# Last two down projections by column halves, the last but one scattered and fetched back in halves

## The chip, the cores and the metric

The kernel runs on one core of a Trainium2 chip, as one program. The metric is device time in microseconds (us), the median over several executions; lower is better. Work is spread over TensorE (PE), VectorE (DVE), ScalarE (ACT) and GpSimd (POOL). SyncE (SP) and POOL issue most of the DMA transfers between DRAM and on-chip memory.

## The reference, cut to what matters

One layer of a hybrid backbone over 128 context and 512 latent tokens of width 1024, all float32. Only its last part, a hierarchical mixture of experts and the final norm, is touched:

```python
# x: (640, 1024) after the mixer; h2 = rmsnorm(x) * (1 + scale2) + shift2
# w_dense (640, 16): top-1 group of 4 experts, then top-2 experts in the group
a = einsum('nd,edf->nef', h2, w_exp_gate)      # 16 experts, 1024 -> 512
u = einsum('nd,edf->nef', h2, w_exp_up)
act = silu(a) * u * w_dense[..., None]
x = x + gate2 * einsum('nef,efd->nd', act, w_exp_down)   # 512 -> 1024
y = rmsnorm(x, g_final)
```

## The kernel before, in words

**Experts.** The 16 experts are visited in the order `expert_at(p)`, p = 0 to 15. Each takes up to 128 tokens (`SLOTS`), gathered by POOL from DRAM (`h2scr`) with an indirect DMA (`gather`). float32 products are made of three products of split numbers (`three`): each weight chunk of 128x2048 is split into a high part by ScalarE (`expert_hi`) and a low part by VectorE (`expert_lo`). An expert has six chunks: four for gate and up (`half`), two for the down projection (`down`), each 1 MB from DRAM. Chunk i can be split once PE has finished chunk i-4. The high copy of p = 15's last chunk (number 95) is the last `expert_hi` of the kernel; the last `expert_lo` follows it on VectorE.

**Down projection.** `down(p)` has FT = 4 blocks of 128 rows. Per chunk (two blocks) it makes 12 products of 128x512: for each block and each of three split products, first the left 512 output columns and then the right 512. So both column halves of the result end together, after the second chunk. `inner_T` of the last expert (a transposition through PE, then `inner_hi` on ScalarE and `inner_lo` on VectorE) is placed between the two chunks of `down(14)`. The result lies in two PSUM banks; ScalarE copies all 128x1024 of it to `yb` (`rows_out`).

**Results.** The result of p = 0 to 14 goes from `yb` to DRAM (`yscr`) by an indirect DMA from POOL (`scatter`). The rows of `yscr` for each token's lower expert are read back as `rowA`, in one transfer of 2.5 MB that POOL issues at p = 13 (line 690). The rows of the upper expert are read back as `rowB` by SP in five transfers of 512 KB (line 549), once the scatter of p = 14 has landed. The result of p = 15 is not needed from DRAM: PE multiplies it with a selection matrix `oh_T` (`last_rows`) and adds `rowB` by an identity product (`second_rows`), tile by tile, t = 0 to 4.

**Tail.** Each engine works through its own queue in the order in which the code writes it, and stops at a wait. ScalarE scales `rowA` by a token weight (`scale_rows`, line 1092). VectorE multiplies it by `gate2` (`base`, line 2011) and adds it to `xr` (`base_add`, line 2016): ten instructions over five tiles, which follow `inner_lo(15)`. Then `combine(t)` (lines 2022, 2025) adds what PE made, ScalarE makes the norm's factor and `finish(t)` (line 2031) applies it; SP writes the tile out.

**ScalarE's order near the end**: `expert_hi(92)`, `(93)`, `tanh_gate(15)`, `inner_hi(14)`, `expert_hi(94)`, `expert_hi(95)`, two copies into `oh_T` (lines 1125, 1126), `inner_hi(15)`, then a wait for the token weights and for `rowA` (`d_ga`), `scale_rows` of t = 0 and 1, `rows_out(14)`, `scale_rows` of t = 2 to 4, `rows_out(15)`.

Of the kernel before, what the change touches and what calls it, by code (L numbers as in the profile page):

```python
# [14 lines left out]
I32 = mybir.dt.int32  # L15
# [5 lines left out]
P = 128  # L21
# [187 lines left out]
def layer_kernel(nc, x_d, small_d, wst_d, wg_d, wpool_d, st_d, rcnt_d,  # L209
                 wexp_d, xt_d, gf_d, bv_d, y_d, so_d, mo_d):  # L210
    ctx = ExitStack()
    with ctx:
# [166 lines left out]
        thr = at("thr", 206, [P, 8])  # L379
        slot_rows = at("slot_rows", 206.0625, [P, 2, NE], I32)  # L380
# [18 lines left out]
        def f32(t):  # L399
# [37 lines left out]
        e_hi, e_lo, e_mm, e_th, e_act, e_part, e_aTp, e_aTh, e_aTl, e_xT, e_xgh, e_xgl, e_y = (  # L437
            sem(n) for n in ("e_hi", "e_lo", "e_mm", "e_th", "e_act", "e_part", "e_aTp", "e_aTh",
# [4 lines left out]
        g_sent, f_ps, s_lt = sem("g_sent"), sem("f_ps"), sem("s_lt")  # L443
        a_steps, v_steps, g_steps = sem("act_steps"), sem("dve_steps"), sem("pool_steps")
# [28 lines left out]
        def _(sp):  # L473
# [47 lines left out]
            with sp.Fori(0, last_round) as r:  # L521
# [40 lines left out]
        def _(gp):  # L562
# [94 lines left out]
            def scatter(r, p):  # L657
                if p:
                    gp.wait_ge(d_sc, r * (16 * NE) + 16 * p)
                    gp.sem_inc(y_sent, 1)  # L660
                if p == NE - 1:
                    for t in range(NT):
                        gp.wait_ge(d_gb[t], (r + 2) * 16)
                gp.wait_ge(e_y, r * NE + p + 2)
                gp.sem_inc(p_go, 1)
                e = expert_at(p)
                gp.indirect_dma_start(yscr, bass.IndirectOffsetOnAxis(
                    ap=slot_rows[:, 1, e:e + 1], axis=0), yb[p % 2][:, :], None).then_inc(d_sc, 16)
                if p == NE - 2:
# [29 lines left out]
        def _(act):  # L699
# [360 lines left out]
            with act.Fori(0, last_round) as r:  # L1060
# [28 lines left out]

                def scale_rows(ts):  # L1090
                    for t in ts:
                        act.activation(rowA[:, t, :], rowA[:, t, :], ACT.Copy,
                                       scale=wab[:, 0, t:t + 1]).then_inc(f_a, 1)

                for t in range(NT):
                    act.wait_ge(d_gb[t], (r + 1) * 16)
# [8 lines left out]
                for p in range(NE):  # L1105
# [8 lines left out]
                    expert_hi(c + 2)  # L1114
                    expert_hi(c + 3)
# [40 lines left out]
        def _(dve):  # L1156
# [682 lines left out]
            with dve.Fori(0, last_round) as r:  # L1839
# [126 lines left out]
                for p in range(NE):  # L1966
# [98 lines left out]
        def _(pe):  # L2065
# [509 lines left out]
            with pe.Fori(0, last_round) as r:  # L2575
# [58 lines left out]
                def down(p, between=None):  # L2634
                    pe.wait_ge(e_aTl, r * NE + p + 1)
                    if p < NE - 1:
                        pe.wait_ge(e_y, r * NE + p + 1)
                    for c in range(2):
# [9 lines left out]
                        if between is not None and c == 0:  # L2648
                            between(p + 1)

                pe.wait_ge(e_y, r * NE + 1)
# [34 lines left out]
                down(NE - 2, inner_T)  # L2686
                down(NE - 1)
# [9 lines left out]
            def second_rows(t):  # L2697
                pe.wait_ge(d_gb[t], rounds * 16 + 16)
# [144 lines left out]
```

## Time and profile before

| | |
|---|---|
| median of 3 runs | 946.25 us (945.71 to 946.47) |
| the profiled execution's own time | 948.32 us |
| its span in the profile | 946.3 us |
| PE busy | 924.8 us, 98% of the span |
| VectorE, ScalarE, GpSimd busy | 746.2, 498.0, 78.8 us |
| granted PE clock, mean | 0.993 of full speed |

The span runs from the first to the last instruction of one profiled execution; the execution's own time is 2.0 us more than it. All times below are us from the span's start.

### The profile page before, as it was taken

How to read it: one execution, taken by the hardware profiler on the slowest of the kernel's cores; microseconds unless marked ns; L12 is line 12 of the kernel's file. 1: busy time of each engine (PE TensorE's matmuls, PEld its weight loads, DVE VectorE, ACT ScalarE, POOL GpSimd, SP SyncE). 2: the span in 40 equal slices, each digit the busy share in tenths (PEclk: the TensorE clock that was granted, in tenths of full speed). 3: DMA queues.
4: the chain of work that ended last, by engine and by line, in shares of the span. 5: the costliest groups of instructions: out<-in, count | busy, mean ns of one | idle time of the engine just before them, and what ended most of it. 6: DMA issues, size and time to landing. Idle time of an engine off the chain costs nothing.

```text
span 946.3 us, 14234 instructions
## 1 busy us (share of the span) xinstructions
PE 924.8 (98%) x5550; PEld 815.4 (86%) x5550; DVE 746.2 (79%) x1038; ACT 498.0 (53%) x660; POOL 78.8 (8%) x91
## 2 busy tenths in 40 slices
PE   7999999999999999999999999989999999999996
PEld 5799999899888999999999998868888888888872
DVE  5798889897494478889464465489999999999998
ACT  5464343343133356576312232257887887887873
POOL 0010110100001010101000000011112111111110
PEclk9999999999999999999999999999999999999998
DMA  9916675574656242434392136179999999999965
GB/s 367 357 60 193 216 231 204 177 266 157 223 198 210 82 127 76 139 124 149 135 358 77 62 125 275 68 257 411 397 422 421 420 407 422 418 410 414 397 265 201
DMA packets 41458, 234.63 MB, mean 248 GB/s; under 512 B 4560, under 2 KB 5008, under 8 KB 20912
## 3 DMA queue, kind: packets, MB, share of 16 engines
q1 hardware_dynamic: 26928, 180.12, 49.5%
q0 software_dynamic: 10720, 44.32, 13.2%
q10 hardware_dynamic: 3744, 9.28, 2.6%
q8 instruction: 44, 0.72, 0.3%
q14 instruction: 22, 0.18, 0.1%
HBM read 208.43 MB, written 25.28 MB: 247 GB/s over the span
## 4 chain that ended last, share of the span: by engine, by line
PE 92%; DVE 4%; DMA 2%; ACT 1%; issue 1%; SPq 0%; DVEq 0%; POOLq 0%; ACTq 0%
PE ps L2067 86%; PE ps L2127 2%; PE ps L2588 1%; DMA raw<-in_wst 1%; PE ps L2630 1%; PE ps L2114 1%; DMA xg<-h2scr,slot_rows 0%; PE ps L2314 0%; PE ps L2425 0%; DVE rowA L2022 0%; DVE xr L2025 0%; DVE xr L2031 0%; PE ps L2502 0%; DVE RP L1359 0%; ACT ghi L774 0%
## 5 line engine op out<-in xcount | busy, mean ns | idle before, releaser
L1848 DVE TENSOR_TENSOR wlo<-raw,whi 128x2048 fp32r<-128x2048 f32 x32 | 72.5, 2289 | 4.2 <-ACT whi L1066 4.0
L1848 DVE TENSOR_TENSOR olo<-raw,ohi 128x2048 fp32r<-128x2048 f32 x32 | 72.4, 2287 | 3.9 <-ACT ohi L1066 3.9
L2067 PE MATMUL ps<-Thi,ghi 128*128 128x320 f32 x224 | 71.1, 317 | 0.0
L1066 ACT ACTIVATE whi<-raw 128x2048 fp32r<-128x2048 f32 x32 | 61.3, 1918 | 18.4 <-PE ps L2067 18.4
L1066 ACT ACTIVATE ohi<-raw 128x2048 fp32r<-128x2048 f32 x32 | 61.3, 1917 | 18.0 <-PE ps L2067 18.0
L2067 PE MATMUL ps<-Tlo,ghi 128*128 128x320 f32 x224 | 69.5, 310 | 0.0
L707 ACT ACTIVATE whi<-raw 128x2048 fp32r<-128x2048 f32 x14 | 26.8, 1912 | 69.7 <-PE ps L2067 69.7
L2067 PEld LDWEIGHTS ps<-Thi,ghi 128*128 128x128 f32 x224 | 42.3, 189 | 11.7 <-issue 10.9
L2067 PE MATMUL ps<-hhi,ghi 128*128 128x320 f32 x168 | 52.3, 311 | 0.0
L2067 PE MATMUL ps<-hlo,ghi 128*128 128x320 f32 x168 | 52.2, 311 | 0.0
L2067 PE MATMUL ps<-hhi,whi 128*128 128x320 f32 x224 | 51.4, 310 | 0.0
L2067 PE MATMUL ps<-hhi,wlo 128*128 128x320 f32 x224 | 51.1, 309 | 0.0
L2067 PE MATMUL ps<-whi,xgh 128*128 128x512 f32 x128 | 50.6, 396 | 0.3 <-ACT xgh L1103 0.3
L2067 PE MATMUL ps<-ohi,xgh 128*128 128x512 f32 x128 | 50.7, 396 | 0.0
L2067 PE MATMUL ps<-ohi,xgl 128*128 128x512 f32 x128 | 50.0, 390 | 0.0
L2067 PE MATMUL ps<-wlo,xgh 128*128 128x512 f32 x128 | 49.8, 389 | 0.0
L2067 PE MATMUL ps<-olo,xgh 128*128 128x512 f32 x128 | 49.8, 389 | 0.0
L2067 PE MATMUL ps<-hlo,whi 128*128 128x320 f32 x224 | 49.7, 309 | 0.0
L2067 PE MATMUL ps<-hhi,owh 128*128 128x320 f32 x160 | 49.3, 324 | 0.1
L2067 PE MATMUL ps<-whi,xgl 128*128 128x512 f32 x128 | 49.0, 390 | 0.0
L2067 PE MATMUL ps<-hhi,owl 128*128 128x320 f32 x160 | 46.9, 309 | 0.0
L2067 PE MATMUL ps<-hlo,owh 128*128 128x320 f32 x160 | 46.9, 309 | 0.0
(450 smaller groups left out, 2653.8 us busy)
## 6 DMA issues: line engine op xcount, KB each, us to landing
raw<-in_wexp SPq DMA_DIRECT2D x64, 1024.0 KB, 8.5
raw<-in_wst SPq DMA_DIRECT2D x59, 1024.0 KB, 6.0
eraw<-in_wexp SPq DMA_DIRECT2D x32, 1024.0 KB, 9.1
thscr<-gout ACTq DMA_DIRECT2D x20, 320.0 KB, 5.2
nm<-negscr POOLq DMA_DIRECT2D x8, 640.0 KB, 6.8
wib<-wiscr POOLq DMA_DIRECT2D x8, 512.0 KB, 5.9
TH<-thscr POOLq DMA_DIRECT2D x3, 1280.0 KB, 6.3
xT<-in_x SPq DMA_DIRECT2D x4, 640.0 KB, 5.8
```

Of the source, the lines that this page charges most:

```text
L707: act.activation(dst[:, :], raw[raw_slot(c)][:, :], ACT.Copy).then_inc(hi_ready, 1)
L1066: act.activation(ehi[i % ESPL][:, :], eraw[s][:, :], ACT.Copy).then_inc(e_hi, 1)
L1848: dve.tensor_tensor(elo[i % ESPL][:, :], eraw[s][:, :], f32(ehi[i % ESPL][:, :]), ALU.subtract).then_inc(e_free[s], 1)
L2067: return nc.tensor.matmul(out, lhsT, rhs, start=start, stop=stop)
L2114: last = nc.tensor.matmul(ps[32 * g:32 * g + 32, 4, 0:2 * P], csil[:, kk, :], raw[slot][:, kk * 2 * P:(kk + 1) * 2 * P], start=kk < 4, sto ...
L2127: last = nc.tensor.matmul(ps[32 * g:32 * g + 32, 7, :], csil[:, k, :], raw[slot][:, g * 512:(g + 1) * 512], start=k == 0, stop=k == KT - 1 ...
L2588: last = nc.tensor.transpose(ps[:, 6 + k // 4, (k % 4) * P:(k % 4 + 1) * P], xg[b][:, k * P:(k + 1) * P], ident)
L2630: last = nc.tensor.transpose(ps[:, 2 * (p % 2), f * P:(f + 1) * P], act_[:, f * P:(f + 1) * P], ident)
```

## The change

The products of `down(14)` and `down(15)` are put in another order (`down_halves`): all 12 products of the left 512 columns over both chunks, then all 12 of the right ones, so the left half of the result is complete halfway through. Both chunks and their splits are now waited for before the first product. `inner_T(15)` stays in the middle of `down(14)`. ScalarE copies each of the two results in two halves of 128x512 (`rows_half`). POOL scatters p = 14 in two indirect transfers, whose row numbers, two new columns `half_rows`, VectorE computes at p = 1. SP reads the first two tiles of `rowB` back in halves: the left ones after the first scatter, the right ones after the second; tiles 2 to 4 whole as before. PE multiplies the left halves of tiles 0 and 1 (`last_rows(0, 0)`, `last_rows(1, 0)`) before it waits for the right half of p = 15's result. On ScalarE the scaling of `rowA`'s tile 0, with the waits for the token weights and for `rowA` in front of it, is moved from behind `inner_hi(15)` to between `expert_hi(94)` and `expert_hi(95)`; tile 1 comes between the halves of p = 14, tiles 2 and 3 before p = 15's first half, tile 4 between its halves. `base` and `base_add` stay on VectorE, in the same order.

```diff
 # SP
-                sp.wait_ge(d_sc, r * (16 * NE) + 16 * (NE - 1))
-                for t in range(NT):
+                sp.wait_ge(d_half, r * 16 + 16)
+                for a in range(2):
+                    if a:
+                        sp.wait_ge(d_sc, r * (16 * NE) + 16 * (NE - 1))
+                    n = slice(a * 512, (a + 1) * 512)
+                    for t in range(2):
+                        sp.dma_start(rowB[:, t, n], yscr[1 + T + t * P:1 + T + (t + 1) * P, n])\
+                          .then_inc(d_gb[t], 16)
+                for t in range(2, NT):
 # POOL, scatter(r, p) for p == NE - 2
+                    for a, done in ((0, d_half), (1, d_sc)):
+                        if a:
+                            gp.wait_ge(e_y, r * (NE + 2) + NE + 1)
+                            gp.sem_inc(p_go, 1)
+                        gp.indirect_dma_start(yscr.rearrange("r (a n) -> (r a) n", a=2),
+                                              bass.IndirectOffsetOnAxis(ap=half_rows[:, a:a + 1], axis=0),
+                                              yb[p % 2][:, a * 512:(a + 1) * 512], None).then_inc(done, 16)
 # ScalarE
+                def rows_half(p, a):
+                    y, n = yb[p % 2], slice(a * 512, (a + 1) * 512)
+                    if a == 0:
+                        act.wait_ge(y_sent, r * NE + p + 1)
+                        act.wait_ge(e_down_half, 2 * r + p - NE + 3)
+                    else:
+                        act.wait_ge(e_mm, r * RCH + down_at(p) + 2 + ESPL)
+                    act.activation(y[:, n], ps[:, DOWN_BANK[p] + a, :], ACT.Copy).then_inc(e_y, 1)
...
                     expert_hi(c + 2)
+                    if p == NE - 1:
+                        act.wait_ge(s_wab, r + 1)
+                        act.wait_ge(d_ga, r * 16 + 16)
+                        scale_rows(range(1))
                     expert_hi(c + 3)
...
                 inner_hi(NE - 1)
-                act.wait_ge(s_wab, r + 1)
-                act.wait_ge(d_ga, r * 16 + 16)
-                scale_rows(range(2))
-                rows_out(NE - 2)
-                scale_rows(range(2, NT))
-                rows_out(NE - 1)
+                rows_half(NE - 2, 0)
+                scale_rows(range(1, 2))
+                rows_half(NE - 2, 1)
+                scale_rows(range(2, 4))
+                rows_half(NE - 1, 0)
+                scale_rows(range(4, NT))
+                rows_half(NE - 1, 1)
 # VectorE, p == 1
                         dve.wait_ge(s_rk_tab, 2 * r + 3)
+                        e = NE + expert_at(NE - 2)
+                        for a in range(2):
+                            dve.tensor_scalar(half_rows[:, a:a + 1], ps[:, 5, e:e + 1], 2.0, float(a), ALU.mult, ALU.add)
 # PE
+                    w = [chunk(down_at(p)), chunk(down_at(p) + 1)]
+                    for a in range(2):
+                        for c in range(2):
+                            hi, lo = w[c]
+                            for f2 in range(2):
+                                f = 2 * c + f2
+                                last = three([(ps[:, DOWN_BANK[p] + a, :], lambda x, a=a, f2=f2:
+                                               x[:, (2 * f2 + a) * 512:(2 * f2 + a + 1) * 512])],
+                                             aTh[p][:, f, :], aTl[p][:, f, :], hi, lo, f == 0, f == FT - 1)
+                            if a:
+                                last.then_inc(e_mm, 1)
+                        if a == 0:
+                            last.then_inc(e_down_half, 1)
+                            if between is not None:
+                                between(p + 1)
...
-            pe.wait_ge(e_y, rounds * NE + 1)
+            pe.wait_ge(e_y, rounds * (NE + 2))
             last_rows(0, 0)
+            last_rows(1, 0)
+            pe.wait_ge(e_y, rounds * (NE + 2) + 1)
             last_rows(0, 1)
-            last_rows(1, 0)
             second_rows(0)
             last_rows(1, 1)
             second_rows(1)
```

## Rows read from the trace of the kernel before

**Rows 1.** The page's chain that ended last, shares of the span by engine

```profile
PE 92%; DVE 4%; DMA 2%; ACT 1%; issue 1%; SPq 0%; DVEq 0%; POOLq 0%; ACTq 0%
```

**Rows 2.** That chain in order of time: start, length, what

```profile
918.51 1.03 ACT yb L1086
919.58 4.70 PE ps L2067 x10
```

**Rows 3.** Timeline of VectorE, 900 to 926: start, length, instruction, [idle before <-releaser]

```profile
909.17 2.29 DVE L1848 TENSOR_TENSOR olo<-eraw,ohi 128x2048 fp32r<-128x2048 f32 x1
911.38 0.68 DVE L1870 TENSOR_TENSOR aTl_last<-ps,aTh_last 128x512 fp32r<-128x512 f32 x1
911.98 2.36 DVE L2011 TENSOR_TENSOR rowA<-rowA,gate 128x1024 f32<-128x1024 f32 x2
...
921.06 2.35 DVE L2016 TENSOR_TENSOR xr<-xr,rowA 128x1024 f32<-128x1024 f32 x2
924.39 1.28 DVE L2022 SCALAR_TENSOR_TENSOR rowA<-ps,wab,gate 128x1024 f32<-128x1024 f32 x1 [0.97 <-PE ps L2067]
```

**Rows 4.** Timeline of ScalarE, 900 to 926

```profile
904.41 1.92 ACT L1066 ACTIVATE ohi<-eraw 128x2048 fp32r<-128x2048 f32 x1 [0.86 <-PE ps L2067]
907.13 1.92 ACT L1066 ACTIVATE ohi<-eraw 128x2048 fp32r<-128x2048 f32 x1 [0.80 <-PE ps L2067]
...
909.43 0.27 ACT L1126 ACTIVATE oh_T<-ps 128x128 f32<-128x128 f32 x1
910.30 0.60 ACT L1080 ACTIVATE aTh_last<-ps 128x512 fp32r<-128x512 f32 x1 [0.60 <-PE ps L2630]
910.79 2.18 ACT L1092 ACTIVATE rowA<-rowA,wab 128x1024 f32<-128x1024 f32 x2
913.07 1.03 ACT L1086 ACTIVATE yb<-ps 128x1024 f32<-128x1024 f32 x1
```

**Rows 5.** The load of rowA: its issue in POOL's timeline, its landing by tile

```profile
882.66 0.94 POOL L690 DMA_DIRECT2D rowA<-yscr  x1
...
DMA to landing us min/median/max: 25.3/25.3/25.3
```

**Rows 6.** The first gather: POOL's issue, shortest landing of tile xg, PE's start

```profile
627.72 1.03 POOL L654 DMA_INDIRECT xg<-h2scr,slot_rows  x1 [3.54 <-DVE slot_rows L1957]
...
DMA to landing us min/median/max: 4.6/7.0/10.1
...
632.34 1.09 PE L2588 MATMUL ps<-small,xg 128*128 128x128 f32 x8 [0.58 <-DMA xg<-h2scr,slot_rows]
```

**Rows 7.** Scatter of p = 14, fetch of rowB, who waits, landings of rowB

```profile
914.89 1.42 POOL L667 DMA_INDIRECT yscr<-yb,slot_rows  x1 [14.47 <-ACT yb L1086]
...
918.67 2.42 SPq L549 DMA_DIRECT2D rowB<-yscr  x5
...
922.28 0.30 PEld L2067 LDWEIGHTS ps<-rowB,small 128*128 128x128 f32 x2 [0.69 <-DMA rowB<-yscr]
...
DMA to landing us min/median/max: 3.6/5.3/6.9
```

**Rows 8.** Timeline of PE: first products of down(15), then last_rows and second_rows(0)

```profile
912.87 0.61 PE L2067 MATMUL ps<-ohi,aTh_last 128*128 128x512 f32 x2
...
919.58 2.84 PE L2067 MATMUL ps<-yb,oh_T 128*128 128x512 f32 x6 [1.11 <-ACT yb L1086]
922.28 1.98 PE L2067 MATMUL ps<-rowB,small 128*128 128x512 f32 x4
```

**Rows 9.** VectorE around the slot numbers at p = 1, and PE's weight loads behind

```profile
654.88 0.17 DVE L1976 CAST slot_rows<-ps 128x24 int32<-128x24 f32 x1
654.97 0.16 DVE L1939 TENSOR_REDUCE thr<-rk_all 128x1 f32<-128x16 f32 x1
...
657.93 0.68 DVE L1870 TENSOR_TENSOR aTl<-ps,aTh 128x512 fp32r<-128x512 f32 x1
...
658.90 0.30 PEld L2067 LDWEIGHTS ps<-whi,aTh 128*128 128x128 f32 x2
```

**Rows 10.** One stretch: us, busy time of each engine, clock, DMA share, GB/s

```profile
882.66:907.96 25.30, 25.30 (x124) 21.09 (x122) 24.11 (x18) 19.84 (x15) 2.51 (x3) 1.00 1.00 403
```

More of the change, by code:

```diff
@@ L379, in layer_kernel @@
         thr = at("thr", 206, [P, 8])
+        half_rows = at("half_rows", 6.9375, [P, 2], I32)
         slot_rows = at("slot_rows", 206.0625, [P, 2, NE], I32)
@@ L436, in layer_kernel @@
         e_free = [sem(f"e_free{s}") for s in range(ERAW)]
-        e_hi, e_lo, e_mm, e_th, e_act, e_part, e_aTp, e_aTh, e_aTl, e_xT, e_xgh, e_xgl, e_y = (
-            sem(n) for n in ("e_hi", "e_lo", "e_mm", "e_th", "e_act", "e_part", "e_aTp", "e_aTh",
+        e_hi, d_half, e_mm, e_th, e_act, e_part, e_aTp, e_aTh, e_aTl, e_xT, e_xgh, e_xgl, e_y = (
+            sem(n) for n in ("e_hi", "d_half", "e_mm", "e_th", "e_act", "e_part", "e_aTp", "e_aTh",
                              "e_aTl", "e_xT", "e_xgh", "e_xgl", "e_y"))
@@ L443, in layer_kernel @@
         g_sent, f_ps, s_lt = sem("g_sent"), sem("f_ps"), sem("s_lt")
+        e_down_half = sem("e_down_half")
         a_steps, v_steps, g_steps = sem("act_steps"), sem("dve_steps"), sem("pool_steps")
@@ L659, in scatter @@
                     gp.wait_ge(d_sc, r * (16 * NE) + 16 * p)
+                    if p == NE - 1:
+                        gp.wait_ge(d_half, r * 16 + 16)
                     gp.sem_inc(y_sent, 1)
@@ L662, in scatter @@
                     for t in range(NT):
-                        gp.wait_ge(d_gb[t], (r + 2) * 16)
-                gp.wait_ge(e_y, r * NE + p + 2)
+                        gp.wait_ge(d_gb[t], (2 * r + 3) * 16 if t < 2 else (r + 2) * 16)
+                gp.wait_ge(e_y, r * (NE + 2) + (p + 2 if p < NE - 1 else NE + 3))
                 gp.sem_inc(p_go, 1)
                 e = expert_at(p)
-                gp.indirect_dma_start(yscr, bass.IndirectOffsetOnAxis(
-                    ap=slot_rows[:, 1, e:e + 1], axis=0), yb[p % 2][:, :], None).then_inc(d_sc, 16)
-                if p == NE - 2:
+                if p != NE - 2:
+                    gp.indirect_dma_start(yscr, bass.IndirectOffsetOnAxis(
+                        ap=slot_rows[:, 1, e:e + 1], axis=0), yb[p % 2][:, :], None).then_inc(d_sc, 16)
+                else:
[6 more added lines that the diff above has]
+                                              yb[p % 2][:, a * 512:(a + 1) * 512], None).then_inc(done, 16)
                     gp.wait_ge(g_sent, 2 * r + 2)
@@ L1095, in _ @@
                 for t in range(NT):
-                    act.wait_ge(d_gb[t], (r + 1) * 16)
+                    act.wait_ge(d_gb[t], (2 * r + 1) * 16 if t < 2 else (r + 1) * 16)
                 for i in range(4):
@@ L1114, in _ @@
                     expert_hi(c + 2)
+                    if p == NE - 1:
+                        act.wait_ge(s_wab, r + 1)
+                        act.wait_ge(d_ga, r * 16 + 16)
+                        scale_rows(range(1))
                     expert_hi(c + 3)
@@ L2632, in inner_T, with down @@
                     last.then_inc(e_aTp, 1)
-                def down(p, between=None):
+                def down(p):
                     pe.wait_ge(e_aTl, r * NE + p + 1)
-                    if p < NE - 1:
-                        pe.wait_ge(e_y, r * NE + p + 1)
+                    pe.wait_ge(e_y, r * (NE + 2) + p + 1)
                     for c in range(2):
@@ L2647, in down, with down_halves @@
                         last.then_inc(e_mm, 1)
-                        if between is not None and c == 0:
-                            between(p + 1)
-                pe.wait_ge(e_y, r * NE + 1)
+                def down_halves(p, between=None):
+                    pe.wait_ge(e_aTl, r * NE + p + 1)
+                    if p < NE - 1:
+                        pe.wait_ge(e_y, r * (NE + 2) + p + 1)
+                    w = [chunk(down_at(p)), chunk(down_at(p) + 1)]
[13 more added lines that the diff above has]
+                                between(p + 1)
+                pe.wait_ge(e_y, r * (NE + 2) + 1)
                 for t in range(NT):
@@ L2685, in _ @@
                         down(p - 1)
-                down(NE - 2, inner_T)
-                down(NE - 1)
+                down_halves(NE - 2, inner_T)
+                down_halves(NE - 1)
                 pe.wait_ge(s_cnt, 1)
@@ L2697, in second_rows @@
             def second_rows(t):
-                pe.wait_ge(d_gb[t], rounds * 16 + 16)
+                pe.wait_ge(d_gb[t], rounds * 32 + 16 if t < 2 else rounds * 16 + 16)
                 for a in range(2):
```

1 line of the change is left out of this document (added).

## Prediction, made before the changed kernel was run

> **What bounds the kernel now.** I read the page first, then the chain that ended last, then the queue of each engine over the last 45 us, then the landings of the transfers that meet there. On the chain PE has 92% of the span [rows 1]. Until 918.5 it consists of PE products, with no gap. There it leaves PE: ScalarE copies the last result whole (1.03 us), and PE takes ten instructions, from 919.58 to 924.28 [rows 2]. From 924.39 VectorE holds the chain to the end. So only two things can move the end: a stall of PE before 918.5, and the start of `combine(0)`, at 924.39 [rows 3]. Behind that point VectorE works without a pause that PE or a transfer causes, so what moves `combine(0)` moves the end by as much.
>
> `combine(0)` waits for two things. PE's sums for tile 0 come last: VectorE sat idle for 0.97 us before it, put down to PE [rows 3]. But right behind this is VectorE's own base work. It starts at 911.98, directly after `inner_lo(15)` (911.38, 0.68 us), runs ten instructions without a gap and ends at 921.06 + 2.35 = 923.41 [rows 3]. From this the reader can see both limits of the change. If PE came much earlier, `combine(0)` could still start only at about 923.45, a gain of at most 0.94 us. And the base work has just 0.94 us of slack: if it starts later than that, it is the bound.
>
> **The change, part by part.**
>
> *PE's end.* Today PE waits 1.11 us for the copy of the whole result, and the weight loads of `second_rows(0)` wait 0.69 us for `rowB` [rows 7, 8]; the products themselves start at 922.28. With halves, the left copy is made during the right products. PE goes from the last product straight to `last_rows(0, 0)` and `last_rows(1, 0)`. Six instructions of `last_rows` take 922.28 - 919.58 = 2.7 us including the short wait, the four of `second_rows(0)` 1.98 us [rows 8]. If nothing upstream moves, tile 0's sums are ready at 918.5 + 2.6 + 2.0 = 923.1 in place of 924.3, 1.2 us earlier. The products themselves cost nothing more: as many of the same shape, each with its own weight load already.
>
> *The wait that is added.* This is the step on which my forecast rests. `scale_rows` of tile 0 now stands before `expert_hi(95)` and brings its wait for `rowA` along. POOL issues this load at 882.66 and it lands 25.3 us later, at 907.96 [rows 5]. That the 25.3 us count from the start of the issue is seen at the first gather: issue 627.72, landing after 4.6 us, so 632.32, and PE, which waits for it, starts at 632.34 [rows 6]. In the kernel before this lateness cost nothing, because ScalarE reached the wait only at 910.79 [rows 4]. In the changed kernel it reaches it when `expert_hi(94)` ends, at 904.41 + 1.92 = 906.33, and stands for 1.6 us. Then comes the scaling, 2.18 / 2 = 1.09 us [rows 4]. `expert_hi(95)` starts at 907.96 + 0.02 + 1.09 = 909.07 in place of 907.13 [rows 4]: 1.94 us later. Only 0.80 us of the old gap was there to hide the scaling in, and the wait fills more than that.
>
> *What is queued behind it.* `expert_lo(95)` on VectorE starts at 909.17 now, 0.12 us after the high copy ends [rows 3, 4], so it moves to 911.0 or 911.1. `inner_hi(15)`, now at 910.30 after 0.60 us of waiting, can run only behind `expert_hi(95)` and the two copies of `oh_T`, which now end at 909.70 [rows 4]; it moves to about 911.6 and ends at 912.2. `inner_lo(15)` follows `expert_lo(95)` directly and moves from 911.38 to about 913.3, ending at 913.95. PE starts `down(15)` at 912.87 now [rows 8]. It needs both the low copy of chunk 95 (which is now wanted before the first product, not the seventh) and `inner_lo(15)`, so it starts at about 913.95: a stall of 1.1 us. Its last product then ends at 918.5 + 1.1 = 919.6, which is where `last_rows` begins today, and the sums of tile 0 are ready at about 924.2, as now: the gain of the halves is spent.
>
> *The base work* moves by the same 1.9 us, from 911.98 to 913.9, and ends at 923.41 + 1.9 = 925.3. The scalings of tiles 1 to 4 (1.09 us each, between half copies) stay ahead of it: tile 1 is scaled by 913.6, needed at 915.1. So the base work ends last. `combine(0)` starts at 925.35 in place of 924.39: **0.95 us later**, and the tail follows. The bounds of this term: 0.85, if the low copy starts the moment the high one ends, and 1.0 with no overlap between VectorE's instructions.
>
> *Scatter and fetch.* The left half of p = 14 is complete at about 909.9, but its copy is queued behind `inner_hi(15)`, so it is made at about 912.1, and POOL issues its scatter near 913.4 (the copy ended at 914.10 and POOL started at 914.89, 0.79 us of delay [rows 4, 7]) and is busy for 1.42 us. The right half is copied when PE ends `down(14)`, at about 913.6, and its scatter starts at about 914.8, as the whole one does now. From issue to SP's first fetch 3.78 us pass now [rows 7]. I take the same for the half, the upper bound; a copy of half the bytes may save a little. So SP issues the right halves of tiles 0 and 1 from 918.6. The shortest landing of a 512 KB fetch is 3.6 us [rows 7]; with that, tile 0 is there by 922.2, just when PE wants it (919.6 + 2.6). Even 1 us more is hidden behind the base work. The two additional fetch issues (2.42 / 5 = 0.48 us each [rows 7]) go out for the left halves before 918. The price of this part is 0. The Trainium skill ("DMA: Bandwidth & Descriptors", Anatomy of one DMA) gives a fixed part of about 2 us per transfer plus bytes at 436 GB/s; by that a half of 256 KB costs an estimated 2.6 us against 3.2 us for 512 KB, so cutting transfers in two gains little. The trace's 3.78 and 3.6 us are for whole ones only, and the sum would be the same by either.
>
> *Two small instructions at p = 1.* They stand before the conversion at 654.88. The next small one starts 0.09 us after it [rows 9]; small instructions of their own length take 0.17. So 0.18 to 0.35 us are added on a busy VectorE. The next work that PE wants from it is the `aTl` part that ends at 657.93 + 0.68 = 658.61; PE loads the weights behind that wait at 658.90 [rows 9], 0.29 us later. Cost 0 to 0.1 us; I take 0.
>
> *Sum.* 948.32 (own time of the profiled execution) + 0.95 = 949.3, and its span 946.3 + 0.95 = 947.25. The profiled execution was 2.07 us above the median of the runs, so the median should be 946.25 + 0.95 = **947.2 us**.
>
> **The rivals.**
>
> *A. As above, ScalarE stands behind `rowA`:* +0.95 us, 947.2. Within it the landing may differ by some tenths. Chance 0.58.
>
> *B. `rowA` is there in time, faster than before.* Then the scaling fills the 0.80 us gap, `expert_hi(95)` starts 0.3 us late, the base work at most 0.2 us late. PE's sums are ready at 923.1, and `combine(0)` starts at 923.45 + 0.2 = 923.65: -0.75 us, 945.5. What decides is the landing: it must be before 906.3 for this, and a landing at 907.96 - 0.95 = 907.0 is the point of no change. Against it stands the measured landing, and nothing before 882.66 is changed. For it: the runs without a profile are 2 us shorter, and the landing in them is not seen. The Trainium skill ("DMA: Bandwidth & Descriptors", Queues, rings and completion order) has each DMA engine take turns between the queues. In this kernel's numbers: 403 GB/s were moved between 882.66 and 907.96 [rows 10]; half of it, 201 GB/s, would carry the load's 2.62 MB in 13 us, to about 896, and the time would be B's. The trace says 25.3 us [rows 5], so I don't follow it. Chance 0.16.
>
> *C. `rowA` later still,* at about 909: the base work then starts 1 us later again, +1.9 us, 948.2. The stretch up to 907.96 has DMA share 1.00 [rows 10], so another order of packets could do it. Chance 0.12.
>
> *D. The fetch is the bound.* If two scatters in a row cost one issue more (1.42 us [rows 7]) and the right half's fetch comes only at 920.1, tile 0 lands at 923.7, PE's sums at 925.7: +1.4 us, 947.7. It decides when tile 0 lands after 923.3. Chance 0.05.
>
> *E. The two effects cancel* (landing near 907.0): within 0.3 us, 946.25. Chance 0.09.
>
> **How the numbers follow.** The likeliest is A, 947.2; its own range is 946.8 to 947.8. B to the low side is 945.5 and C to the high side 948.2; a range that leaves out no more than 2 in 10 must hold B's middle and most of C, with 0.3 us for the spread of a median (the runs before spread over 0.76 us): 945.3 to 948.5. A difference of 0.2% is 1.9 us, about what a measurement of this kernel can tell from no change. A, B, D and E all lie within it: 0.88, less small tails. C lies on its edge, half of it slower. Slower 0.10, faster 0.04 (a gain above 0.94 us is excluded by the base work unless that starts earlier too), same 0.86.
>
> **What the profile would show.** Right: an idle time of ScalarE of about 1.6 us at 906.3 before the first `scale_rows`, ended by the DMA of `rowA`; `expert_hi(95)` near 909.1; an idle time of PE of about 1.1 us before `down(15)`; VectorE's base work from 913.9 to 925.3 and no idle time before `combine(0)`. PE would not wait between the last product and `last_rows`, and not for `rowB`. Wrong: if the first `scale_rows` starts at 906.3, B holds. If VectorE idles before `combine(0)` with PE waiting for `rowB`, D does. If PE idles near 658.7, the small instructions cost something.

## The result, and the profile after

The changed kernel took 948.97 us (median of 19 runs, 946.96 to 950.36), the kernel before in the same series 946.98 (19 runs, 945.71 to 948.44). The ratio is 1.002, with 1.0013 to 1.0026 as its 95% interval: slower, and on the edge of the 0.2% at which the prediction drew its line. Its profiled execution took 949.89 us with a span of 947.8. The forecast was 947.2, and its range ended at 948.5. The direction was right and the size was not. The sections below find that the last 45 us did what was predicted to within 0.3 us, that the base to which the sum was added was 0.7 to 1.2 us too low, and that 1.3 us of the distance to the measured median are not in those 45 us at all.

ScalarE's timeline of the changed kernel, 900 to 921 (start, length, instruction, idle time before it and what ended that), answers to [rows 4]:

```profile
904.76 1.92 ACT L1085 ACTIVATE ohi<-eraw 128x2048 fp32r<-128x2048 f32 x1 [0.86 <-PE ps L2103]
908.26 1.16 ACT L1120 ACTIVATE rowA<-rowA,wab 128x1024 f32<-128x1024 f32 x1 [1.58 <-DMA rowA<-yscr]
909.32 1.89 ACT L1085 ACTIVATE ohi<-eraw 128x2048 fp32r<-128x2048 f32 x1
...
911.75 0.60 ACT L1099 ACTIVATE aTh_last<-ps 128x512 fp32r<-128x512 f32 x1
912.23 0.61 ACT L1116 ACTIVATE yb<-ps 128x512 f32<-128x512 f32 x1
...
919.97 0.60 ACT L1116 ACTIVATE yb<-ps 128x512 f32<-128x512 f32 x1 [1.08 <-PE ps L2103]
```

The reader is to see the second row: ScalarE stands idle for 1.58 us, released by `rowA`'s DMA, between the high copies of the last two chunks. This execution runs 0.35 us later than that of before from the first gather on (904.76 against 904.41), which its PE waited for a little longer, so stretches are best read from the start of `expert_hi(94)`. From there `expert_hi(95)` is at 4.56 us, before at 2.72: 1.84 later.

VectorE's timeline, which answers to [rows 3]:

```profile
911.24 2.29 DVE L1881 TENSOR_TENSOR olo<-eraw,ohi 128x2048 fp32r<-128x2048 f32 x1 [1.64 <-ACT ohi L1085]
913.45 0.68 DVE L1903 TENSOR_TENSOR aTl_last<-ps,aTh_last 128x512 fp32r<-128x512 f32 x1
914.05 2.35 DVE L2047 TENSOR_TENSOR rowA<-rowA,gate 128x1024 f32<-128x1024 f32 x2
...
923.13 2.35 DVE L2052 TENSOR_TENSOR xr<-xr,rowA 128x1024 f32<-128x1024 f32 x2
925.52 1.28 DVE L2058 SCALAR_TENSOR_TENSOR rowA<-ps,wab,gate 128x1024 f32<-128x1024 f32 x1
```

The idle time has moved. Before, VectorE waited 0.97 us in front of `combine(0)`; now it waits 1.64 us in front of `expert_lo(95)`, and the base work runs straight into `combine(0)`.

PE's timeline, which answers to [rows 8]:

```profile
914.19 0.50 PE L2103 MATMUL ps<-ohi,aTh_last 128*128 128x512 f32 x1 [0.82 <-DVE aTl_last L1903]
...
919.77 2.74 PE L2103 MATMUL ps<-yb,oh_T 128*128 128x512 f32 x6
922.34 1.88 PE L2103 MATMUL ps<-rowB,small 128*128 128x512 f32 x4
```

PE waits before `down(15)`, for VectorE's `aTl_last`. Behind that it waits for nothing: neither for a copy (1.11 us before) nor for `rowB` (0.69 us).

POOL's and SP's timelines, which answer to [rows 7]:

```profile
913.62 0.97 POOL L686 DMA_INDIRECT yscr<-yb,half_rows  x1 [12.86 <-ACT yb L1116]
915.14 0.97 POOL L686 DMA_INDIRECT yscr<-yb,half_rows  x1 [0.55 <-issue]
```

```profile
916.46 2.47 SPq L555 DMA_DIRECT2D rowB<-yscr  x4
918.97 1.38 SPq L558 DMA_DIRECT2D rowB<-yscr  x3
```

The first row of SP groups both pairs; the right one goes out from 918.13, so 2.99 us pass from the issue of the right scatter to it, against 3.78 for a whole one.

The chain that ended last, in order of time (start, length, what), shows the whole mechanism; before, PE held it until 918.5 [rows 2]:

```profile
883.01 25.16 DMA rowA<-yscr
...
909.32 1.90 ACT ohi L1085
911.24 1.19 DVE olo L1881
...
913.45 0.68 DVE aTl_last L1903
914.14 1.22 DVE rowA L2047 x2
...
923.22 2.28 DVE xr L2052 x2
925.52 1.29 DVE rowA L2058
```

### The profile page after: what moved, and what is told of

Same layout as the page of the kernel before. It is cut to its first block, busy times and chain, and to the rows that moved or that the text cites. A ratio compares the mean times of both kernels' runs of the same rounds, so it can differ in the third digit from the quotient of the medians.

```text
span 947.8 us, 14248 instructions
## 1 busy us (share of the span) xinstructions
PE 924.8 (98%) x5550; PEld 815.8 (86%) x5550; DVE 746.5 (79%) x1040; ACT 497.8 (53%) x662; POOL 78.7 (8%) x92
## 4 chain that ended last, share of the span: by engine, by line
PE 84%; DVE 6%; DMA 5%; issue 3%; ACT 2%; SPq 0%; DVEq 0%; POOL 0%; ACTq 0%; POOLq 0%
PE ps L2103 78%; DMA rowA<-yscr 3%; DMA raw<-in_wst 1%; PE ps L2624 1%; PE ps L2163 1%; PE ps L2150 1%; ACT ghi L793 1%; PE ps L2666 1%; DMA xg<-h2scr,slot_rows 1%; DVE rowA L2047 1%; PE ps L2350 0%; PE ps L2461 0%; DVE RP L1392 0%; DVE rowA L2058 0%; DVE xr L2061 0%
## 5 line engine op out<-in xcount | busy, mean ns | idle before, releaser
L2103 PEld LDWEIGHTS ps<-Thi,ghi 128*128 128x128 f32 x224 | 42.1, 188 | 11.7 <-issue 10.9
```

Source lines behind the costliest of these rows:

```text
L2103: return nc.tensor.matmul(out, lhsT, rhs, start=start, stop=stop)
```

## The experiments

Two measures are used. The *local* one is the time from the start of `expert_hi(94)` to that of `combine(0)` in a trace. It leaves out all that lies before the change, and the tail: from `combine(0)` to the end of the span all 17 traces take 21.9 or 22.0 us, but for the first one of the changed kernel with 22.3, whose last output ends later. The other is the median, with the recorded ratio to the kernel before in the same series and its 95% interval; this ratio is not the quotient of the two medians, and the two differ by up to 0.13%. The four series' medians of before were 947.39 (30 runs), 947.59 (27), 946.79 (35) and 947.84 (29). All kernels below also read the count of rounds on VectorE at p = 8, with its bounds stated, in place of behind the loop:

```diff
+                        rounds = dve.value_load(rounds_i[0:1, 0:1], min_val=1, max_val=ROUNDS)
...
-            rounds = dve.snap(last_round, min_val=1, max_val=ROUNDS)
```

**control** is the kernel before with this alone.

> The kernel before with nothing but the bounded count of rounds at p = 8, which all these experiments have. Theory: its load is hidden in VectorE's slack; no difference that can be measured, expert_hi(94) to combine(0) 20.0 to 20.2. Rival: it costs its 0.5 us on the path and the other results have to be read against it.

Measured: 947.71 (11 runs), 1.0006 (0.9997 to 1.0015); local 20.02 us, before 19.98. It costs nothing that can be measured.

**after_again, after_more, after_4** are the changed kernel again, with no further edit.

> The changed kernel, but VectorE's count of rounds is read a second time at p = 8 with its bounds stated, the way PE reads it (an extra small load, hidden in VectorE's slack). The theory (ScalarE stands 1.6 us for rowA, base work 1.9 us late, combine(0) at most 1.0 us late): about +1 us against the kernel before in the trace. The measured median says +2.0 us: if that holds here again, about 1 us of it is not in the theory, and the landing of rowA or the end of the span must show it. The rival, spread of the runs: +1 us this time.

> The changed kernel again (with the bounded count of rounds). Two series put it 2.0 and 1.4 us above the kernel before, while the traces put combine(0) only 0.6 to 0.8 us later. The spans fall in groups about 1.5 us apart, by whether the granted clock of PE dips near 172 and near 618 us, which lies before everything that the change touches. Theory (chance mix of dips): this time the difference of the medians is near 0.8 us and no more than half of the runs have a mean clock of 0.994 or less. Rival (the stall of PE before down(15) brings a further loss that the single trace doesn't show): again 1.5 us or more, with a clock below that of the control.

> The changed kernel once more. Over 38 runs its mean is 1.3 us above that of 92 runs of the kernel before, its traces show 0.6 to 0.8 us at combine(0); the mean clock is 0.994 or less in 21 of 38 runs against 26 of 92. Theory (chance mix of the two early dips of the clock): the difference of the means is 0.5 to 1.2 us, and at most 4 in 10 runs have a mean clock of 0.994 or less. Rival (the changed kernel meets the dips more often): 6 in 10 such runs again, and 1.3 us or more.

Measured: 948.81 (8 runs), 1.0020 (1.0007 to 1.0033); 948.64 (11), 1.0011 (1.0001 to 1.0022); 947.22 (12), 1.0001 (0.9992 to 1.0009). The local time hardly moved: 20.61, 20.77 and 20.81 us, after 20.76 in the first trace; `rowA`'s wait was 1.42, 1.59 and 1.62 us. So the stall at the end is nearly the same each time, while the whole time's distance from before wanders. after_more's expectation is met by the means (0.87 us apart) and the low clocks (4 of 11), and missed by the medians, which were 1.85 us apart.

**move_alone, move_again**: the kernel before with only the scaling of tile 0 and its two waits moved.

```diff
                     expert_hi(c + 2)
+                    if p == NE - 1:
+                        act.wait_ge(s_wab, r + 1)
+                        act.wait_ge(d_ga, r * 16 + 16)
+                        scale_rows(range(1))
                     expert_hi(c + 3)
...
-                act.wait_ge(s_wab, r + 1)
-                act.wait_ge(d_ga, r * 16 + 16)
-                scale_rows(range(2))
+                scale_rows(range(1, 2))
```

> The kernel before with one edit: the scaling of rowA's tile 0 and its waits stand before expert_hi(95); nothing is halved. Theory: ScalarE stands 1.6 us for rowA, base work starts 1.9 us late, PE's down(15) 1.1 us late and its sums for tile 0 at 925.4, so combine(0) at 925.4: +1.0 us. Rival (the loss lies in the halves): within 0.2 us of the kernel before.

> The kernel before with the moved scaling alone, once more; it has the same stall of PE before down(15) (1.0 us) as the changed kernel. Theory: 1.1 us slower by the trace, and as often a low mean clock as the kernel before (3 in 10). Rival (a stall there brings low clocks more often): 6 in 10, and 1.6 us or more slower.

Measured: 947.93 (11 runs), 1.0007 (0.9998 to 1.0016), and 947.64 (11), 1.0005 (0.9997 to 1.0014); local 21.17 and 20.73 us. ScalarE's and VectorE's timelines of the first:

```profile
907.97 1.15 ACT L1092 ACTIVATE rowA<-rowA,wab 128x1024 f32<-128x1024 f32 x1 [1.79 <-DMA rowA<-yscr]
...
925.43 1.28 DVE L2024 SCALAR_TENSOR_TENSOR rowA<-ps,wab,gate 128x1024 f32<-128x1024 f32 x1 [0.23 <-PE ps L2069]
```

The move by itself brings the stall and the whole local loss (+0.7 to +1.1 us; move_again, for which 1.1 was expected, has the smaller one, with a wait of 1.35 us for `rowA`). The halves can give back no more than the last 0.23 us, because the base work is the bound.

**scale_back**: the changed kernel, with the scaling and its waits put back behind `inner_hi(15)`.

```diff
-                    if p == NE - 1:
-                        act.wait_ge(s_wab, r + 1)
-                        act.wait_ge(d_ga, r * 16 + 16)
-                        scale_rows(range(1))
...
                 inner_hi(NE - 1)
+                act.wait_ge(s_wab, r + 1)
+                act.wait_ge(d_ga, r * 16 + 16)
+                scale_rows(range(1))
```

> The changed kernel with the scaling of rowA's tile 0 and its two waits put back behind inner_hi(15); halves, two scatters and seven fetches stay. Theory: no wait before expert_hi(95), which starts at 907.1; no stall of PE before down(15); base work from 912.0 to 923.4, combine(0) at 923.5, so 0.9 us faster than the kernel before and 1.9 us faster than the changed one. Rival (the halves, the doubled scatter or the wait for both chunks cost the time): still slower than before by 1 us or more.

Measured: 947.4 (11 runs), 1.0002 (0.9992 to 1.0012). ScalarE does not wait for `rowA` any more, nor PE before `down(15)`. But there is a new wait, and the 0.9 us that were expected are not there. PE's timeline, VectorE's, POOL's and SP's:

```profile
921.32 1.98 PE L2102 MATMUL ps<-rowB,small 128*128 128x512 f32 x4 [1.65 <-DMA rowB<-yscr]
```

```profile
923.42 1.28 DVE L2057 SCALAR_TENSOR_TENSOR rowA<-ps,wab,gate 128x1024 f32<-128x1024 f32 x1 [0.99 <-PE ps L2102]
```

```profile
911.84 0.97 POOL L686 DMA_INDIRECT yscr<-yb,half_rows  x1 [12.80 <-ACT yb L1116]
913.37 1.96 POOL L686 DMA_INDIRECT yscr<-yb,half_rows  x1 [0.55 <-issue]
```

```profile
914.67 4.74 SPq L555 DMA_DIRECT2D rowB<-yscr  x4
919.45 1.38 SPq L558 DMA_DIRECT2D rowB<-yscr  x3
```

The right half's fetch goes out at 918.61, 5.24 us after its scatter's issue (913.37), not 3.0, and PE waits 1.65 us for it. Local time 20.38 us: 0.3 us worse than before, although the stall is gone.

**tile0_first**: `rowA` loaded in two transfers, tile 0 first, with its own count, which the first scaling waits for; the scaling of tile 1 waits for the rest.

```diff
-                        gp.dma_start(rowA[:, :, :], yscr[1:1 + T, :].rearrange(
+                        gp.dma_start(rowA[:, 0, :], yscr[1:1 + P, :]).then_inc(d_pool, 16)
+                        gp.dma_start(rowA[:, 1:NT, :], yscr[1 + P:1 + T, :].rearrange(
...
-                        act.wait_ge(d_ga, r * 16 + 16)
+                        act.wait_ge(d_pool, D_ZERO + r * 16 + 16)
...
+                act.wait_ge(d_ga, r * 16 + 16)
                 scale_rows(range(1, 2))
```

> The changed kernel, but POOL issues rowA in two transfers, tile 0 (512 KB) first with a count of its own, tiles 1 to 4 behind it; ScalarE waits before expert_hi(95) for tile 0 alone. Theory: tile 0 lands long before 906.3, the scaling fills the old 0.8 us gap, expert_hi(95) starts at 907.4, combine(0) at 923.7: 0.75 us faster than the kernel before. Rival (it is the added 1.09 us instruction or another part that costs, not the wait): no faster than before.

Measured: 947.29 (11 runs), 1.0002 (0.9993 to 1.0011), local 20.21 us. Tile 0 landed after 12.3 us, and ScalarE did not wait: `expert_hi(95)` starts 2.86 us after `expert_hi(94)`, 0.14 later than before. PE waited 1.48 us for `rowB`, and of the 0.75 us that were expected nothing is there.

**load_early**: the changed kernel with the load of `rowA` issued right behind the wait in `scatter(12)`, which came out 11.7 us earlier and not the 17 us of the expectations. **load_late**: issued at p = 14.

```diff
+                    if p == 12:
+                        gp.dma_start(rowA[:, :, :], yscr[1:1 + T, :].rearrange(
+                            "(t p) d -> p t d", p=P)).then_inc(d_ga, 16)
...
-                    if p == 13:
-                        gp.dma_start(rowA[:, :, :], yscr[1:1 + T, :].rearrange(
-                            "(t p) d -> p t d", p=P)).then_inc(d_ga, 16)
```

> The changed kernel with one edit beside the bounded count of rounds: POOL issues the load of rowA 17 us earlier, in front of the scatter of p = 12 (the rows of the lower experts are complete by then). Measured from the start of expert_hi(94) to combine(0), the kernel before has 19.98 us, the changed one 20.76. Theory: no idle time of ScalarE for rowA, the scaling fits the 0.8 us gap; if rowB were there this would give 19.2. The runs so far make a late rowB likely: 20.2, PE waiting 1.5 us for it, so 0.2 us slower than before and 0.5 to 0.8 us faster than the changed kernel. Rival (the load is late for another reason than the moment of its issue): ScalarE waits again and 20.7.

> The changed kernel with rowA's load issued by POOL one expert later, behind the scatter of p = 13, to double the wait: it should land some 3.8 us later than in the changed kernel, since the weights' queue is empty from 907 on. Theory (the moved wait holds chunk 95's split, inner_hi(15), PE and the base work, one for one): combine(0) 24 to 25 us after expert_hi(94) starts, 4 to 5 us slower than the kernel before. Rival (the wait is covered and the loss lies elsewhere): below 22 us.

Measured, early: 946.62 (11 runs), 0.9996 (0.9987 to 1.0005); local 20.00 us. `rowA` is issued at 871.27 and lands 22.4 us later, so nobody waits for it, and again PE waits for `rowB`. SP's right fetch goes out at 917.77, 5.27 us behind the scatter's issue:

```profile
912.50 1.89 POOL L689 DMA_INDIRECT yscr<-yb,half_rows  x1 [0.38 <-issue]
```

```profile
920.36 1.98 PE L2103 MATMUL ps<-rowB,small 128*128 128x512 f32 x4 [1.27 <-DMA rowB<-yscr]
```

Measured, late: 955.78 (4 runs), 1.0093 (1.0078 to 1.0109); local 29.05 us. ScalarE waited 8.20 us for `rowA` and PE stood still for 7.45 us before `down(15)`. Against before that is 9.1 us, twice the 4 to 5 expected: `rowA`'s landing moved by 6.6 us and not by 3.8, and PE adds a loss of its own. The local time grew by 8.3 us over the changed kernel's, but `rowA`'s wait by only 6.6; `combine(0)` waits the other 1.70 us for PE. The stretches of the trace behind the stall (us, busy time of PE, PEld, VectorE, ScalarE and POOL, granted clock, DMA share, GB/s) show why PE is the later one:

```profile
915.00:918.00 3.00, 0.00 (x0) 0.00 (x0) 2.79 (x2) 3.00 (x7) 0.40 (x1) 0.50 0.00 0
918.00:921.00 3.00, 2.84 (x7) 2.26 (x8) 3.00 (x4) 2.40 (x3) 1.70 (x3) 0.50 0.35 132
921.00:924.00 3.00, 3.00 (x9) 2.32 (x8) 3.00 (x4) 0.31 (x1) 0.00 (x0) 0.50 0.84 261
924.00:927.00 3.00, 3.00 (x13) 2.28 (x12) 3.00 (x3) 1.54 (x3) 0.00 (x0) 0.95 0.93 295
```

The granted clock is 0.50, the 1.2 GHz level, and stays there until about 924. `down(15)` took 8.4 us instead of 5.6. The 0.82 us stall of the changed kernel brought no such fall.

**early_late_fetch, elf_again**: load_early, and `rowB` fetched whole, in five transfers after both scatters, as before the change.

```diff
-                for a in range(2):
-                    if a:
-                        sp.wait_ge(d_sc, r * (16 * NE) + 16 * (NE - 1))
-                    n = slice(a * 512, (a + 1) * 512)
-                    for t in range(2):
-                        sp.dma_start(rowB[:, t, n], yscr[1 + T + t * P:1 + T + (t + 1) * P, n])\
-                          .then_inc(d_gb[t], 16)
-                for t in range(2, NT):
+                sp.wait_ge(d_sc, r * (16 * NE) + 16 * (NE - 1))
+                for t in range(NT):
```

> As load_early, and SP fetches rowB whole, in five transfers, only after both scatters of p = 14 have landed (the scatters stay halved, the left one early). Theory: the left fetches ran in the DMA queues beside the right scatter and delayed it from 3.8 to 5 us; without them it lands within 3.3 us of POOL's issue, tile 0 is there 3.6 us later, PE hardly waits, and combine(0) starts 19.3 us after expert_hi(94) starts: 0.7 us faster than the kernel before. Rival (the halved scatter is slow by itself, whatever runs beside it): rowB as late as in load_early, 20.2 or more.

> The version with the early load of rowA and rowB fetched whole after both scatters, once more, to halve its interval. Theory from its trace (combine(0) 19.52 us after expert_hi(94) starts, the kernel before 20.0): 0.5 us faster than the kernel before in the mean, 1.2 us faster than the changed one. Rival: no faster than the kernel before.

Measured: 946.78 (11 runs), 0.9995 (0.9985 to 1.0005), and 947.07 (11), 0.9995 (0.9986 to 1.0004); local 19.52 and 19.50 us, half a microsecond less than before, both times. The first execution's rows:

```profile
916.43 2.46 SPq L552 DMA_DIRECT2D rowB<-yscr  x5
```

```profile
922.18 1.28 DVE L2052 SCALAR_TENSOR_TENSOR rowA<-ps,wab,gate 128x1024 f32<-128x1024 f32 x1 [0.48 <-PE ps L2097]
```

The fetch is issued 3.73 us behind the right scatter (912.70), and lands early enough that VectorE idles only 0.48 us before `combine(0)`. In the second execution it did not idle at all. Over the 22 runs the mean is 0.49 us below that of before (0.45 ± 0.31 us at the same mean clock) and 1.5 us below that of the changed kernel. Against before each interval still holds no change; it is the best of the kernels tried, by the trace more than by the time.

**early_t0_half**: load_early with only tile 0's left half fetched ahead (`range(1)` in place of `range(2)` in the fetch of the halves). **early_whole**: the kernel before with the move and the early load, nothing halved.

> As load_early, but only the left half of tile 0 of rowB is fetched between the two scatters (one transfer of 256 KB in place of two); its right half follows the right scatter, tiles 1 to 4 whole. Theory (each early transfer delays the right scatter in the DMA queues, and a half fetched last lands a microsecond sooner than a whole): the right scatter lands 4.3 us after POOL's issue, tile 0 some 2.6 us later, combine(0) 19.2 us after expert_hi(94) starts: 0.8 us faster than the kernel before. Rival (any early fetch costs the right scatter its full delay): 20.0 as load_early.

> The kernel before with the scaling of tile 0 moved before expert_hi(95) and rowA's load issued 17 us earlier; nothing is halved. Theory: no wait for rowA, and nothing won either, since combine(0) is bound by the whole copy of p = 15, by rowB (fetched at the same moment as before) and PE's order: 20.0 from expert_hi(94) to combine(0), and the same time as before. What load_early and early_late_fetch gain against it belongs to the halves. Rival (the earlier load is worth something by itself): 0.3 us or more faster.

Measured: 948.16 (11 runs), 1.0012 (1.0002 to 1.0021), local 19.73 us, PE's wait for `rowB` 0.98 us; and 948.16 (12 runs), 1.0027 (1.0004 to 1.0051), local 20.16 us. The first was expected 0.8 us faster than before and measured slower, though its trace is 0.3 us faster locally; the profiled execution had both of the clock falls described below, and the rest is open. Two of the second one's twelve executions took 957.35 and 957.67 us, and its interval is wide through them; what they met is open. Without the halves the early load is worth nothing locally (20.16 against a mean of 20.06 for the three traces with before's code at the end).

**p1_ops_alone**: the kernel before with the two new instructions at p = 1.

```diff
+                        e = NE + expert_at(NE - 2)
+                        for a in range(2):
+                            dve.tensor_scalar(half_rows[:, a:a + 1], ps[:, 5, e:e + 1], 2.0, float(a), ALU.mult, ALU.add)
```

> The kernel before with the two small instructions for half_rows at p = 1 alone. Theory: 0.13 us on VectorE, hidden in front of down(0); no difference in the time, and 19.98 from expert_hi(94) to combine(0). Rival (part of the measured 2 us comes from here): 0.3 to 1 us slower than the kernel before.

Measured: 946.89 (11 runs), 0.9995 (0.9986 to 1.0005). They cost nothing that can be measured.

## Why the prediction was right about the place and wrong about the size

*The added wait: right.* It was put at 1.6 us, ending with `rowA` 25.3 us after its issue; it is 1.58 us, with a landing after 25.16. `expert_hi(95)` was to be 1.94 us later and is 1.84; PE was to stall for 1.1 us at `down(15)`. `down(15)` starts 0.97 us later relative to `expert_hi(94)` ((914.19 - 904.76) - (912.87 - 904.41)), of which the row marks 0.82 as waiting. move_alone shows that this stall is caused by the move, and scale_back, tile0_first and load_early, each taking its cause away in another manner, that it goes with it.

*The base work ends last: right.* The gap that VectorE had before `combine(0)` is gone, and PE's sums do not decide.

*The size of the local term: 0.95 predicted, 0.68 measured.* The mean of the four traces of the changed kernel is 20.74 us, that of the three with before's code at the end (before, control, p1_ops_alone) 20.06. The 0.27 us are made of small things: the wait was 0.1 us cheaper, the low copy starts 0.03 us after the high one ends (911.24 against 909.32 + 1.89) and not 0.12, and before's own profiled execution, from which I took the gap, lies 0.08 us below the mean of its like.

*Scatter and fetch, price 0: right here, for the wrong reason in B.* In the changed kernel PE doesn't wait for `rowB`; the half's scatter to fetch took 2.99 us, less than the 3.78 that I allowed. *The two instructions at p = 1: right*, at no measurable cost.

*Rival B: its condition was right, its price was not.* I gave -0.75 us for `rowA` in time. Three kernels with all the halves take the wait away (scale_back, tile0_first, load_early) and none gains: local 20.38, 20.21 and 20.00 us, +0.3 to -0.1. B took PE's sums at 923.1 as if `rowB` were there by then, but the fetch had been worked out only against A's end, which hides it. What takes the place of the wait is D's mechanism, a late fetch. early_late_fetch tells what makes it late: with no left half fetched between the scatters the right scatter's data come 3.73 us after the issue, with the two left fetches 5.27 (load_early), the issue 1.89 us long in both, and the half microsecond appears. But the left fetches are not the whole condition, since the changed kernel has them too and needs 2.99 us.

What decides is whose packets come first on the DMA engines. Queue q0 carries POOL's transfers, q1 SP's (packets, MB, share of the 16 engines). The changed kernel, 916.60 to 917.40, 1.5 to 2.3 us behind the right scatter's issue:

```profile
q0 software_dynamic: 71, 0.26, 85.4%
```

load_early, 914.90 to 916.10 (2.4 to 3.6 us behind it), then 916.10 to 917.40:

```profile
q1 hardware_dynamic: 78, 0.16, 69.5%
```

```profile
q1 hardware_dynamic: 145, 0.26, 53.0%
q0 software_dynamic: 80, 0.26, 49.6%
```

early_late_fetch, 915.10 to 916.10 (2.4 to 3.4 us behind it):

```profile
q0 software_dynamic: 80, 0.26, 68.7%
```

The 0.26 MB of the right half move in about 0.8 us when nothing stands in front. In load_early the left fetches' packets come first; the scatter's begin 1.1 us later than in early_late_fetch and take 1.3 us. All nine traces with a left fetch fall in line. Where the left fetch is issued after POOL's issue of the right scatter has ended (the four of the changed kernel and load_late), the scatter's packets come first and the right fetch follows the issue by 2.8 to 3.0 us. Where it is issued before that end (scale_back, tile0_first, load_early, early_t0_half), the fetch's packets come first and it takes 4.4 to 5.3 us. In the first three of these POOL's issue was the long one, 1.9 us. In early_t0_half it was short, 1.02 us, but the left fetch went out only 0.57 us behind its start, and the right one 4.4 us. So a long issue isn't needed for the loss; it is one way in which the fetch comes first. What makes the issue long stays open.

*The failed step is the base of the sum, in "How the numbers follow" and "Sum".* "The median should be 946.25 + 0.95", with "0.3 us for the spread of a median". The base was three runs. In the series of the result the kernel before took 946.98 us; over 140 runs (the 19 of this series, which hold those three, and 121 of the other four) the mean is 947.4 us, 1.2 us higher, and one run's standard deviation is 1.0 us (1.2 for the changed kernel). With 947.4 as base and 0.95 the same working gives 948.4. The 1.77 us between 947.2 and 948.97 are 0.73 of base, -0.27 of the local term, and 1.3 that the traces don't show in the last 45 us. The sum had no term for such a part. It took the 2.07 us by which the profiled execution lay above the median as one number to be subtracted, and did not ask what they were. That execution had both falls of the clock described next, and its trace showed them; the first costs 1.6 us. That the three runs had none is likely and not shown, as they have no trace.

The mean of the changed kernel's 50 runs is 948.43; against before's 947.45 that is +0.98 us. If runs are compared at the same mean clock, +0.68 ± 0.24 us remain. That this is the very 0.68 of the traces is in part luck, since the mean clock says only roughly whether a run met a fall that costs time.

*What the spread consists of.* Stretches of the traces long before the change (columns as above). The kernel before:

```profile
170.00:175.00 5.00, 4.47 (x24) 4.47 (x25) 4.70 (x7) 0.61 (x2) 0.00 (x0) 0.73 0.14 53
620.00:625.00 5.00, 4.97 (x21) 3.86 (x22) 4.24 (x22) 3.91 (x3) 0.10 (x1) 0.72 0.95 341
```

The changed kernel, in its first trace:

```profile
170.00:175.00 5.00, 4.55 (x26) 4.55 (x27) 4.63 (x7) 0.60 (x2) 0.00 (x0) 0.78 0.13 50
620.00:625.00 5.00, 4.98 (x21) 3.70 (x20) 4.17 (x22) 3.90 (x3) 0.10 (x1) 0.66 0.97 352
```

after_again, the same work:

```profile
170.00:175.00 5.00, 4.78 (x34) 4.78 (x35) 4.46 (x8) 0.60 (x2) 0.00 (x0) 1.00 0.07 25
620.00:625.00 5.00, 3.01 (x20) 2.28 (x20) 4.15 (x21) 4.99 (x4) 0.10 (x1) 1.00 1.03 410
```

In some executions the clock falls in one or both of these places, in others in neither. In the first place it goes down to 0.50, the 1.2 GHz level, for two or three us (173 to 175 in the kernel before). PE stood idle for 1.21 us shortly before, at 169.3, and for 1.23 us in after_again, where no fall came, so the idle time doesn't tell the two apart. What each costs is read at the first gather, whose issue lies behind both. The changed kernel with both falls, after_more with the first alone, scale_back with the second alone (0.78 from 615 to 620, 0.88 from 620 to 625), after_again with none:

```profile
627.66 1.02 POOL L663 DMA_INDIRECT xg<-h2scr,slot_rows  x1 [3.48 <-DVE slot_rows L1990]
```

```profile
627.49 1.02 POOL L663 DMA_INDIRECT xg<-h2scr,slot_rows  x1 [3.53 <-DVE slot_rows L1990]
```

```profile
626.11 1.03 POOL L663 DMA_INDIRECT xg<-h2scr,slot_rows  x1 [3.30 <-DVE slot_rows L1989]
```

```profile
625.90 1.02 POOL L663 DMA_INDIRECT xg<-h2scr,slot_rows  x1 [3.50 <-DVE slot_rows L1990]
```

Over the 17 traces the gather is issued at 627.4 to 628.1 in the nine with the first fall and at 625.9 to 626.5 in the eight without. The first fall costs 1.6 us. The second costs nothing that can be seen: the four traces that have it alone have the mean of the four that have none (626.2). There PE has idle time to give, as the last row of after_again shows (3.01 us busy of 5). The changed kernel's spans were 947.8 us with both falls, 946.6 with the first alone and 944.9 with none, and of the 1.2 us between the first two 0.2 lie before the gather, 0.6 between it and `expert_hi(94)` and 0.4 behind `combine(0)`. A median over few runs depends on how many of them met the first fall.

*What stays open.* The distance between the means of the two kernels was +1.8, +1.3, +0.9 and +0.1 us over the four series that had the changed kernel. Runs with a mean clock of 0.994 or less were 25 of 50 for it (12 of 19, 5 of 8, 4 of 11, 4 of 12) and 36 of 121 for before. The mean clock is a rough sign, though: move_alone's trace has the costly first fall at a mean of 0.996, load_early's only the costless second one at 0.995. Whether the changed kernel meets the first fall more often, or the first two series had bad luck, isn't settled. Each of the last four series ran on a chip of its own, and before's means on them lie within 0.3 us. The stall itself is no cause that shows: move_alone and move_again have it, and only 3 of their 22 runs had the low clock.

## What to carry to other kernels

An instruction that is moved takes its wait along: look up when the transfer lands, not whether the wait was free where it stood, and count what is queued behind it. Cutting a transfer so that a part can be fetched early has a price where the early fetch's packets come before those of the late part; here, by the traces, the halves were worth most (0.5 us) with the fetch left whole and late, and the load made earlier, and the times of whole runs don't tell that gain from no change. And take the base of a sum from as many runs as the effect needs, since three of them were off by more than the whole effect; where the profiled execution lies 2 us off the others, look for the reason in its clock before the two are treated as one.

## What the runs showed of the hardware that was not expected

TensorE's granted clock fell in two stretches near 172 and 620 us in some executions of a program and not in others. The first fall cost 1.6 us at the first gather, the second nothing that could be seen. After 7.45 us of standing still PE came back at half its clock (0.50) and kept it until about 924, some 6 us; after a stall of 0.82 us it did not fall. The same indirect half scatter held POOL for 0.97 us in some executions and for 1.9 us in others (early_late_fetch 1.89, elf_again 1.01, the same kernel), and its data were ready for SP 3.73 and 2.85 us after the issue. A half scatter whose packets came behind those of a 256 KB fetch was ready only after 4.4 to 5.3 us.
